# A three-block transformer kernel on one core: the experts' down products move into their own block's turn; in the second attention the rotary work goes ahead of the convolution's taps and sigmoid gates become tangents

## The chip, the cores and the metric

The kernel is one program on 1 core of a Trainium2 chip. The metric is the device time of one execution in microseconds (us), lower is better. The core has a matrix engine (TensorE, PE in the rows; PEld is its weight load), a vector engine (VectorE, DVE), an activation engine (ScalarE, ACT), GpSimd (POOL) and SyncE (SP), which here only issues transfers. They run side by side, each in its own written order, and wait for one another by semaphores.

## The reference, cut to what matters

Three transformer blocks stand one after the other on 512 tokens of width 1024. The change touches the mixture of experts of the first block and the attention with its convolution in the second.

```
# first block: mixture of experts
order = jnp.argsort(e_flat)                      # assignments sorted by expert, 32 experts, 2 per token
def run(args):
    xb, e = args
    gate, up = jnp.split(xb @ w_gate_up[e], 2, axis=-1)
    return (jax.nn.silu(gate) * up) @ w_down[e]
y = jax.ops.segment_sum(y_buf[dest] * w_s[:, None].astype(h.dtype), tok_s, num_segments=n_tok)

# second block: projections, attention over 8 heads in blocks of 128 queries, convolution of width 31
z = h @ w_in
c_q, c_kv, k_r, u_glu, gate_logits = jnp.split(z, IN_OFFSETS, axis=-1)
q = (rms_norm(c_q, q_norm) @ w_uq).reshape(B, S, N_HEADS, QK_NOPE_DIM + QK_ROPE_DIM)
q_rope = apply_rope(q[..., QK_NOPE_DIM:], cos[:, :, None, :], sin[:, :, None, :])
s = jnp.einsum('bhqd,bhkd->bhqk', qn_b, k_nope) + jnp.einsum('bhqd,bkd->bhqk', qr_b, k_rope)
p = jax.nn.softmax(s, axis=-1).astype(v.dtype)   # causal mask before it

a, b = jnp.split(u_glu, 2, axis=-1)
u = a * jax.nn.sigmoid(b)
u = lax.conv_general_dilated(u, conv_w, padding=[(CONV_WIDTH - 1, 0)], feature_group_count=CONV_CHANNELS) + conv_b
u = jax.nn.silu(layer_norm(u, conv_ln_g, conv_ln_b))
```

## The kernel before, in words

The kernel is one hand-ordered program for each engine. Every function such as `moe_pe` or `att2_dve` writes out one engine's part of a stage, and its order in the text is the order in which that engine works. A helper records operations for all of them, so the line in a row is often a helper's: L316 to L318 are the three products of a weight tile, L324 general products, L339 transposes, L294 and L302 the high and the low part of a weight tile.

**Weights in two parts.** A weight tile that must be multiplied exactly is split: ACT copies the rounded high part (`act_hi`, L294, tiles ws0h to ws2h), DVE subtracts it from the weight (`dve_lo`, L302, ws0l to ws2l), and PE multiplies high by high, high by low and low by high. `dve_lo` of a tile waits for its `act_hi`, and that waits until PE has finished the tile that held the same buffers.

**Experts.** The 32 experts are taken as 16 blocks of two (`NMAIN`), each expert on 64 rows. A turn of the loop is: gate and up products of block bb (L1535, 32 matmuls from `w` and the gathered tokens in `arena`), with 16 products back to the tokens (L324, `onehot`, `yo_hi`, `yo_lo`) of block bb - 2 between them; 8 transposes of the next block's tokens; silu on ACT (L1612), times up and the routing weight on DVE (L1637), 2 transposes of that on PE (L339 from `t`), a copy on ACT (L1616); then the 16 down products of block bb - 1 (L1535 from `w` and `t`). ACT and DVE split the outcome (L1606, L1628), and DVE adds what comes back to x (L1632). After the loop stand the 8 pairs of products back of block 14, the down products of block 15 and its 8 pairs back. Weights come on SP's queue, in the order gate-up, down, gate-up, down, 2 MB and 1 MB for an expert, into two rings of 5 buffers. A transfer into a ring's buffer waits until the products that last used it are done, and those behind it in the queue wait too.

**Second attention.** Its 32 units are 8 heads of 4 query blocks, i = 3, 2, 1, 0 (512, 384, 256, 128 keys). In step t of 35 PE makes the scores of unit t (L324), turns the probabilities of unit t - 2 (L2018) and multiplies those of unit t - 3 by the values; DVE has the reciprocal and a diagonal for unit t - 1 (L2066, L2069), the maximum for unit t (L2074), then `CONV2` taps of the convolution (L1864; the first tap of a channel group is L1861), then what the fills need, and at i = 0 the rotary part of the next head's query (`head2_dve`, L1981, L1982, L1984), for which the next head's first scores wait. The convolution has 8 groups of 31 taps, 248 in all.

**Fills.** The 16 tiles of u_glu are called fills. PE spreads the 24 matmuls of each over some three steps (L1935). Even fills are the gate's half, which ACT turns into the sigmoid (L1834). Odd fills are the other half, which DVE multiplies with it (L1846). Before an odd fill's product DVE catches up with taps until `31 * (m - 1)` are done. Fills 0 to 3 come ahead of the attention (`p2_pe`), fills 4 to 15 in steps 1, 4, 7, 10, 13, 16, 18, 21, 24, 27, 30 and 33. All those in the attention use one bank, so PE starts a fill only when its predecessor was taken. The taps left after the attention run between the first merge's tiles (`mixN_dve`, `ln_dve`: 20 after tile 0, 20 after tile 1, all the rest after tile 2).

## Time and profile before

| | |
|---|---|
| median of 3 runs | 2996.79 us (2995.47 to 3001.74) |
| profiled execution, its own time | 2995.61 us |
| its span | 2993.6 us |
| mean granted clock of TensorE | 0.943 |
| TensorE busy | 89% of the span |
| VectorE busy | 52% |
| ScalarE busy | 34% |
| expert loop, first gate product to last product back | 630.60 to 926.2 us |
| second attention, first scores to last | 1048.12 to about 1310 us |

A row of the trace gives start and duration in us, engine, line, operation, output and inputs with their shapes, how many instructions are merged in it, and in brackets how long the engine had been idle and what ended that.

### The profile page before, as it was taken

The numbers are of one execution on the slowest core, as the hardware profiler recorded it, in microseconds if no ns is written. First come the engines' busy times: TensorE is split into PE (matmuls) and PEld (weight loads), VectorE is DVE, ScalarE is ACT, GpSimd is POOL, SyncE is SP. The second block draws the span as 40 slices with busy tenths as digits, with TensorE's granted clock in tenths as the row PEclk, the third lists the DMA queues.
The fourth block names the chain that finished last, engine by engine and source line by source line (L and its number), as shares of the span: only waits on it lengthen the run. The fifth ranks groups of instructions, "written<-read, shape, count | busy, mean of one in ns | idle before, by whom it ended". The sixth has DMA issues, their size and how long they took to land.

```text
span 2993.6 us, 29418 instructions
## 1 busy us (share of the span) xinstructions
PE 2677.3 (89%) x11760; PEld 1923.5 (64%) x11760; DVE 1565.7 (52%) x2840; ACT 1010.6 (34%) x1723; POOL 15.8 (1%) x20
## 2 busy tenths in 40 slices
PE   6989998979994989978994999949989999999997
PEld 2566777633432645556873888837768878778786
DVE  5226764457557466778536444475553323343534
ACT  1024454321113322332433333324663334442232
POOL 0000000000000000000000000000000000000000
PEclk9988999989997988989997999979999999999999
DMA  6111002198982200021320232121213143122220
GB/s 176 42 43 31 29 15 85 57 372 358 371 358 84 88 22 15 15 85 56 113 105 35 85 113 85 57 71 61 68 57 113 57 112 86 69 85 85 85 83 31
DMA packets 178749, 295.99 MB, mean 99 GB/s; under 512 B 26160, under 2 KB 120752, under 8 KB 170416
## 3 DMA queue, kind: packets, MB, share of 16 engines
q1 hardware_dynamic: 175088, 282.52, 27.0%
q0 software_dynamic: 2304, 8.39, 0.7%
q10 hardware_dynamic: 1216, 3.15, 0.3%
q8 instruction: 95, 1.56, 0.2%
q14 instruction: 46, 0.38, 0.0%
HBM read 288.79 MB, written 4.19 MB: 98 GB/s over the span
## 4 chain that ended last, share of the span: by engine, by line
PE 54%; DVE 10%; ACT 3%; issue 1%; DVEq 0%; ACTq 0%
PE ps L316 15%; PE ps L318 15%; PE ps L317 15%; PE ps L324 7%; DVE arena L1864 3%; PE ps L1935 2%; DVE t L369 1%; DVE t L353 1%; PE ps L339 1%; DVE t L2186 0%; PE ps L2018 0%; DVE arena L2168 0%; PE ps L1957 0%; ACT L2595 0%; DVE ws0l L302 0%
## 5 line engine op out<-in xcount | busy, mean ns | idle before, releaser
L302 DVE TENSOR_TENSOR ws0l<-w,ws0h 128x1024 fp32r<-128x1024 f32 (+2 forms) x125 | 135.4, 1083 | 128.8 <-ACT ws0h L294 128.5
L302 DVE TENSOR_TENSOR ws1l<-w,ws1h 128x1024 fp32r<-128x1024 f32 (+1 forms) x124 | 137.7, 1110 | 119.1 <-ACT ws1h L294 119.1
L1864 DVE SCALAR_TENSOR_TENSOR arena<-arena 128x512 f32<-128x512 f32 x240 | 180.3, 751 | 7.4
L324 PE MATMUL ps<-arena 128*128 128x512 f32 (+11 forms) x440 | 145.4, 511 | 27.4 <-DVE arena L1984 23.0
L294 ACT ACTIVATE ws0h<-w 128x1024 fp32r<-128x1024 f32 (+2 forms) x125 | 117.8, 943 | 127.8 <-PE ps L318 124.0
L294 ACT ACTIVATE ws1h<-w 128x1024 fp32r<-128x1024 f32 (+1 forms) x124 | 119.4, 963 | 111.4 <-PE ps L318 104.3
L302 DVE TENSOR_TENSOR ws2l<-w,ws2h 128x1024 fp32r<-128x1024 f32 (+1 forms) x94 | 102.1, 1086 | 89.3 <-ACT ws2h L294 89.3
L1535 PE MATMUL ps<-w,arena 128*64 128x512 f32 x512 | 129.5, 643 | 20.4 <-issue 19.0
L324 PE MATMUL ps<-t,con 128*128 128x512 f32 (+1 forms) x68 | 46.1, 773 | 107.3 <-DVE t L353 86.7
L316 PE MATMUL ps<-hpc_hi,ws0h 128*128 128x512 f32 x320 | 128.1, 400 | 6.1 <-DVE ws0l L302 4.0
L316 PE MATMUL ps<-hpc_hi,ws1h 128*128 128x512 f32 x328 | 130.9, 399 | 1.5 <-issue 1.5
L318 PE MATMUL ps<-hpc_hi,ws1l 128*128 128x512 f32 x328 | 128.9, 393 | 0.0
L317 PE MATMUL ps<-hpc_lo,ws1h 128*128 128x512 f32 x328 | 128.7, 392 | 0.0
L316 PE MATMUL ps<-hpc_hi,ws2h 128*128 128x512 f32 x312 | 123.5, 396 | 3.3 <-ACT hpc_hi L1102 2.3
L317 PE MATMUL ps<-hpc_lo,ws0h 128*128 128x512 f32 x320 | 125.2, 391 | 0.0
L318 PE MATMUL ps<-hpc_hi,ws0l 128*128 128x512 f32 x320 | 125.2, 391 | 0.0
L339 PE MATMUL ps<-con,t 128*128 128x128 f32 (+1 forms) x556 | 102.4, 282 | 23.5 <-DVE t L982 7.3
L318 PE MATMUL ps<-hpc_hi,ws2l 128*128 128x512 f32 x312 | 121.6, 390 | 0.0
L317 PE MATMUL ps<-hpc_lo,ws2h 128*128 128x512 f32 x312 | 121.4, 389 | 0.0
L294 ACT ACTIVATE ws2h<-w 128x1024 fp32r<-128x1024 f32 (+1 forms) x94 | 88.7, 944 | 86.3 <-PE ps L318 86.3
L1632 DVE TENSOR_TENSOR x<-x,ps 128x512 f32<-128x512 f32 x128 | 80.4, 681 | 64.8 <-PE ps L324 64.7
L339 PEld LDWEIGHTS ps<-con,t 128*128 128x128 f32 (+1 forms) x556 | 70.7, 142 | 59.6 <-issue 10.7
(533 smaller groups left out, 6142.2 us busy)
## 6 DMA issues: line engine op xcount, KB each, us to landing
w<-in_w_gate_up SPq DMA_DIRECT2D x32, 2048.0 KB, 12.1
w<-in_w_in SPq DMA_DIRECT2D x37, 1024.0 KB, 5.6
w<-in_w_down SPq DMA_DIRECT2D x32, 1024.0 KB, 11.4
w<-in_w_ff SPq DMA_DIRECT2D x16, 2048.0 KB, 8.1
w<-in_w_in SPq DMA_DIRECT2D x13, 2048.0 KB, 7.8
w<-in_w_in SPq DMA_DIRECT2D x48, 512.0 KB, 5.2
w<-in_w_branch SPq DMA_DIRECT2D x6, 2048.0 KB, 7.7
w<-in_w_out SPq DMA_DIRECT2D x4, 2048.0 KB, 7.8
```

The lines of the kernel that those rows point to most:

```text
L294: A_(e).activation(pair_of(t)[0], tiles[t][1], ACT.Copy).then_inc(*e.inc(hi, ("hi", t)))
L302: e.go.tensor_tensor(p[1], tiles[t][1], p[0].bitcast(F32), ALU.subtract).then_inc(*e.inc(lo, ("lo", t)))
L316: e.go.matmul(bank, p[0][:, k, :], high, start=k == 0, stop=False)
L317: e.go.matmul(bank, p[0][:, k, :], low, start=False, stop=False)
L318: i = e.go.matmul(bank, p[1][:, k, :], high, start=False, stop=k == K - 1)
L324: i = e.go.matmul(bank, lt, rt, start=j == 0, stop=j == n - 1)
L339: i = e.go.transpose(dst, src, ident[0:k, 0:k])
L353: e.go.tensor_tensor(N.acc[:], N.acc[:], N.square(k)[:], ALU.add).then_inc(*e.inc(dv, (N.tag, "add", k)))
L1535: i = e.go.matmul(bank[h_, :], rows[:, h_], weights[r], start=start, stop=stop)
L1632: e.go.tensor_tensor(x[:, d, :], x[:, d, :], ps[3 + (8 * bb + d) % 3][:], ALU.add).then_inc(*e.inc(dv, ("xm", bb, d)))
L1864: i = e.go.scalar_tensor_tensor(out=cv[:, m, :], in0=ureg[:, m % 2, k:k + 512], scalar=cw[:, m, k:k + 1], in1=cv[:, m, :], op0=ALU.mult, o ...
L1935: i = e.go.matmul(ps[5][:], p[w_ // 2][:, k, :], hpN[w_ % 2][:, k, :], start=r == 0, stop=r == 23)
```

## The change

The experts' loop gets a different order on PE, ACT and DVE: the two gate transposes come ahead of the next tokens' eight, and the down products are those of the turn's own block. The products back are then those of block bb - 1, and the work after the loop shrinks to one block's. In the second attention the gate's sigmoid becomes a hyperbolic tangent of half the argument: sigmoid(b) = (tanh(b / 2) + 1) / 2, the 1 is added in the product on DVE, and the factor one half goes once into the convolution's weights. On DVE the low part of a weight tile two ahead is made before an odd fill's catch-up and product, the rotary part of the next head stands ahead of the taps, and a step has 6 taps for 5.

```diff
-                behind = {2: (0, 1, 2), 5: (3, 4, 5), 7: (6, 7)} if bb - 2 >= b0 else {}
+                behind = {2: (0, 1, 2), 5: (3, 4, 5), 7: (6, 7)} if bb > b0 else {}
                 for k in range(8):
...
                     for d in behind.get(k, ()):
-                        back(bb - 2, d)
+                        back(bb - 1, d)
+                e.wait_ge(*dv(("up", bb)))
+                turns(e, [(ps[2][:, P * k:P * k + P], tm[bb % 2][:, P * k:P * k + P]) for k in range(2)], ("g", bb))
                 if bb + 1 < b1:
                     turn_x(bb + 1)
-                e.wait_ge(*dv(("up", bb)))
-                turns(e, [(ps[2][:, P * k:P * k + P], tm[bb % 2][:, P * k:P * k + P]) for k in range(2)], ("g", bb))
-                if bb > b0:
-                    down(bb - 1)
-            for d in range(8):
-                back(b1 - 2, d)
-            down(b1 - 1)
+                down(bb)
             for d in range(8):
                 back(b1 - 1, d)
...
-                e.go.activation(sig_of(j)[:], fill_bank(j)[:], ACT.Sigmoid).then_inc(*e.inc(ev, ("fill", j)))
+                e.go.activation(sig_of(j)[:], fill_bank(j)[:], ACT.Tanh, scale=0.5).then_inc(*e.inc(ev, ("fill", j)))
...
             m = j // 2
+            dve_lo(e, fill_t[j] + 2)
             if j % 2:
                 while e.conv < 31 * (m - 1):
                     conv_dve(e, 1)
...
-                e.go.tensor_tensor(ureg[:, m % 2, 30:542], sig_of(j)[:], fill_bank(j)[:], ALU.mult).then_inc(*e.inc(dv, ("fill", j)))
+                e.go.scalar_tensor_tensor(out=ureg[:, m % 2, 30:542], in0=sig_of(j)[:], scalar=1.0, in1=fill_bank(j)[:], op0=ALU.add,
+                                          op1=ALU.mult).then_inc(*e.inc(dv, ("fill", j)))
                 e.inputs = m + 1
-            dve_lo(e, fill_t[j] + 2)
...
+                        e.go.tensor_scalar(cw, cw, 0.5, None, ALU.mult).then_inc(*e.inc(dv, "cw"))
...
-        CONV2 = 5
+        CONV2 = 6
...
+                if t < NU2 and units2[t][1] == 0 and units2[t][0] < 7:
+                    head2_dve(e, units2[t][0] + 1)
                 conv_dve(e, CONV2)
                 for j in fills_at(t):
                     fill_dve(e, j)
-                if t < NU2 and units2[t][1] == 0 and units2[t][0] < 7:
-                    head2_dve(e, units2[t][0] + 1)
```

ACT and DVE follow in the experts' loop: ACT copies the gates before the next tokens and takes the own block's outcome, and DVE makes the matrix back to the tokens (`to_tokens`, L1473, L1476) after its product with up.

On PE, the end of turn 1 of the experts' loop reads so before: the last gate product (weights in buffers `w_51` and `w_52`), the next tokens' transposes, the gates' transposes, then the down products of block 0 (`w_63`, `w_64`).

```order
L1535 MATMUL ps<-w_52,arena 64x512
L339 MATMUL ps<-con,arena 128x128 x8
L339 MATMUL ps<-con,t 128x128 x2
L1535 MATMUL ps<-w_63,t 64x512
L1535 MATMUL ps<-w_64,t 64x512
```

The same place now ends with a product back of block 0 (`onehot_90`), and the down products are those of block 1 (`w_65`, `w_66`).

```order
L324 MATMUL ps<-onehot_90,yo_lo 128x512
L339 MATMUL ps<-con,t 128x128 x2
L339 MATMUL ps<-con,arena 128x128 x8
L1535 MATMUL ps<-w_65,t 64x512
L1535 MATMUL ps<-w_66,t 64x512
```

The two sets of transposes have changed places, and each block's down products stand one turn earlier.

On DVE, steps 27 and 28 of the second attention read so before: the maximum of unit 27 (ISA, 128x128), the taps, the product of fill 13 (L1846), the low part for fill 15, the rotary part of head 7 (L1981 to L1984), the reciprocal and the diagonal, and the maximum of unit 28.

```order
L2074 ISA ps,m<-ps,con 128x128
L2074 ISA m 128x1
L1864 SCALAR_TENSOR_TENSOR arena<-arena 128x512 x6
L1846 TENSOR_TENSOR arena<-t,ps 128x512
L302 TENSOR_TENSOR ws1l<-w_59,ws1h 128x1024
L1981 TENSOR_TENSOR ps<-ps,tabs 64x512
L1982 TENSOR_TENSOR t<-t,tabs 64x512
L1984 TENSOR_TENSOR arena<-t,ps 64x512
L2066 RECIPROCAL m<-m 128x1
L2069 TENSOR_SCALAR tabs<-con,m 128x128
L2074 ISA ps,m<-ps,con 128x512
```

The same steps now (lines of the new file: L1973 to L1976 rotary, L1856 taps, L1834 the fill's product, L2066 the maximum):

```order
L2066 ISA ps,m<-ps,con 128x128
L2066 ISA m 128x1
L1973 TENSOR_TENSOR ps<-ps,tabs 64x512
L1974 TENSOR_TENSOR t<-t,tabs 64x512
L1976 TENSOR_TENSOR arena<-t,ps 64x512
L1856 SCALAR_TENSOR_TENSOR arena<-arena 128x512 x6
L302 TENSOR_TENSOR ws1l<-w_59,ws1h 128x1024
L1834 SCALAR_TENSOR_TENSOR arena<-t,ps 128x512
L2058 RECIPROCAL m<-m 128x1
L2061 TENSOR_SCALAR tabs<-con,m 128x128
L2066 ISA ps,m<-ps,con 128x512
```

The rotary part has moved ahead of the taps, and the fill's product behind the low part.

On ACT, a turn of the experts' loop reads so before: silu, the next block's tokens, the gates' copy, the high part of the down products, the next silu.

```order
L1612 ACTIVATE t<-ps 128x256
L1599 ACTIVATE arena<-ps 128x512 x2
L1616 ACTIVATE t<-ps 128x256
L1606 ACTIVATE yo_hi<-ps 128x512 x2
L1612 ACTIVATE t<-ps 128x256
```

And now, with L1608 for silu, L1610 for the copy, L1595 for the tokens and L1602 for the high part:

```order
L1608 ACTIVATE t<-ps 128x256
L1610 ACTIVATE t<-ps 128x256
L1595 ACTIVATE arena<-ps 128x512 x2
L1602 ACTIVATE yo_hi<-ps 128x512 x2
L1608 ACTIVATE t<-ps 128x256
```

The copy of the gates has moved ahead of the tokens' two copies. In the second block the program before has 7 loads of a table of functions ahead of L1834 and 7 ahead of the exponential (L2043); the new one has a single one, ahead of the first tangent.

## Rows read from the trace of the kernel before

**Rows 1.** Waits of PE, 640 to 930 us: total us, times, longest.

```profile
PE ps L1535 <- issue: 19.0, 9, 3.9
```

**Rows 2.** Timeline of PE in the experts' loop.

```profile
630.60 9.54 PE L1535 MATMUL ps<-w,arena 128*64 128x512 f32 x32 [0.78 <-ACT arena L1599]
...
642.28 7.09 PE L1535 MATMUL ps<-w,arena 128*64 128x512 f32 x32 [0.61 <-ACT t L1616]
...
854.71 3.65 PE L1535 MATMUL ps<-w,t 128*64 128x512 f32 x16
...
870.87 3.65 PE L1535 MATMUL ps<-w,t 128*64 128x512 f32 x16
877.43 4.49 PE L1535 MATMUL ps<-w,arena 128*64 128x512 f32 x12 [2.91 <-issue]
...
895.34 2.74 PE L1535 MATMUL ps<-w,arena 128*64 128x512 f32 x12
```

**Rows 3.** Timeline of all engines at the end of the experts' loop.

```profile
907.41 0.38 ACT L1616 ACTIVATE t<-ps 128x256 f32<-128x256 f32 x1 [1.11 <-PE ps L339]
...
917.36 3.65 PE L1535 MATMUL ps<-w,t 128*64 128x512 f32 x16
...
925.79 0.39 PE L324 MATMUL ps<-onehot,yo_lo 128*128 128x512 f32 x1
```

**Rows 4.** Windows, experts' loop: us, PE, PEld, DVE, ACT, POOL busy, clock, DMA share, GB/s.

```profile
711.00:727.00 16.00, 13.19 (x58) 5.86 (x58) 15.31 (x31) 1.47 (x3) 0.94 (x1) 1.00 0.97 402
...
823.00:837.00 14.00, 14.00 (x66) 6.40 (x64) 10.04 (x22) 2.35 (x5) 0.94 (x1) 1.00 1.02 429
```

**Rows 5.** Transfers, 640 to 900 us.

```profile
DMA packets 9896, 94.21 MB, mean 362 GB/s; under 512 B 1103, under 2 KB 1103, under 8 KB 2767
```

**Rows 6.** Waits of PE, 1048 to 1310 us.

```profile
PE ps L324 <- DVE arena L1984: 23.0, 8, 5.2
PE ps L1935 <- DVE arena L1846: 6.8, 3, 5.6
```

**Rows 7.** Timeline of PE in the attention: first scores of heads 6 and 7.

```profile
1257.64 1.12 PE L324 MATMUL ps<-arena 128*128 128x512 f32 x2 [2.48 <-DVE arena L1984]
...
1291.16 2.07 PE L324 MATMUL ps<-arena 128*128 128x512 f32 x2 [5.22 <-DVE arena L1984]
```

**Rows 8.** The chain of waits, same places: start, us, what.

```profile
1259.81 1.14 PE ps L1935 x4
...
1262.99 1.48 PE ps L324 x4
...
1295.24 2.00 PE ps L1935 x4
```

**Rows 9.** Timeline of DVE in the attention, head 6 to the first merge.

```profile
1282.38 0.30 DVE L2074 CUSTOM_DVE_ANT_0 ps<-ps,con 128x128 f32<-128x128 f32 x1 [3.94 <-PE ps L324]
...
1282.60 4.68 DVE L1864 SCALAR_TENSOR_TENSOR arena<-arena 128x512 f32<-128x512 f32 x6
...
1287.99 1.22 DVE L302 TENSOR_TENSOR ws1l<-w,ws1h 128x1024 fp32r<-128x1024 f32 x1
1289.12 0.68 DVE L1981 TENSOR_TENSOR ps<-ps,tabs 64x512 f32<-64x512 f32 x1
...
1291.04 0.15 DVE L2066 RECIPROCAL m<-m 128x1 f32<-128x1 f32 x1
...
1327.70 1.22 DVE L302 TENSOR_TENSOR ws2l<-w,ws2h 128x1024 fp32r<-128x1024 f32 x1
```

**Rows 10.** Timeline of PE at the first merge and ahead of the attention.

```profile
1034.41 5.53 PE L324 MATMUL ps<-arena,w 128*128 128x512 f32 x12 [1.05 <-DVE arena L1846]
...
1329.07 0.76 PE L316 MATMUL ps<-hpb_hi,ws2h 128*128 128x512 f32 x1 [9.59 <-DVE ws2l L302]
```

**Rows 11.** Timeline of ACT in step 31: a table load for the sigmoid.

```profile
1307.47 0.59 ACT L2052 ACTIVATE arena<-ps 128x512 f32<-128x512 f32 x1
1308.08 1.28 ACT L1834 ACT_TABLE_LOAD   x1
```

More of the change, by code:

```diff
@@ L1612, in moe_act @@
                 e.go.activation(tm[bb % 2][:, 0:256], ps[2][:, 0:256], ACT.Silu).then_inc(*e.inc(ev, ("silu", bb)))
+                e.wait_ge(*tp(("g", bb)))
+                e.go.activation(tm[bb % 2][:, 256:512], ps[2][:, 0:256], ACT.Copy).then_inc(*e.inc(ev, ("g", bb)))
                 if bb + 1 < b1:
                     turned_x(bb + 1)
-                e.wait_ge(*tp(("g", bb)))
-                e.go.activation(tm[bb % 2][:, 256:512], ps[2][:, 0:256], ACT.Copy).then_inc(*e.inc(ev, ("g", bb)))
-                if bb > b0:
-                    high(bb - 1)
+                high(bb)
                 if bb == 6:
                     act_sines(e, "a2", 0)
-            high(b1 - 1)
         def moe_dve(e, b0, b1):
@@ L1644, in moe_dve @@
             for bb in range(b0, b1):
-                old = range(8) if bb - 2 >= b0 else ()
+                old = range(8) if bb > b0 else ()
                 for d in old[0:3]:
-                    add(bb - 2, d)
+                    add(bb - 1, d)
                 if bb + 2 < b1:
@@ L1651, in moe_dve @@
                 for d in old[3:6]:
-                    add(bb - 2, d)
-                if bb > b0:
-                    to_tokens(e, bb - 1)
+                    add(bb - 1, d)
                 up(bb)
                 for d in old[6:8]:
-                    add(bb - 2, d)
+                    add(bb - 1, d)
+                to_tokens(e, bb)
                 if bb + 1 < b1:
                     weights_of(e, bb + 1)
-                if bb > b0:
-                    low(bb - 1)
+                low(bb)
                 if bb == 4:
@@ L1666, in moe_dve @@
                     dve_angles(e, "a2", 0, tm[4][:], tm[4][:], tm[5][:])
-            for d in range(8):
-                add(b1 - 2, d)
-                if d == 2:
-                    to_tokens(e, b1 - 1)
-            low(b1 - 1)
             for d in range(8):
@@ L1859, in conv_dve @@
                     e.wait_ge(*dv(("fill", 2 * m + 1)))
-                    e.wait_ge(*in_cw("cw"))
+                    if m == 0:
+                        e.wait_ge(*in_cw("cw"))
+                        e.go.tensor_scalar(cw, cw, 0.5, None, ALU.mult).then_inc(*e.inc(dv, "cw"))
+                    e.wait_ge(*dv("cw"))
                     i = e.go.tensor_scalar(cv[:, m, :], ureg[:, m % 2, 0:512], cw[:, m, 0:1], vcol("conv_b_2", m), ALU.mult, ALU.add)
```

## The prediction

> **What bounds the kernel now.** I read the busy shares first: TensorE works 89% of the span, so time is made or lost where it stops. Then I read, for the two stages that the change touches, the waits of PE, and the timelines around the longest.
>
> In the experts' loop PE waits 9 times, 19.0 us in all, for something that the waits put down to "issue" [rows 1]. The name says little; the place says more. The waits stand ahead of the first gate product of a block, which waits for the weights to land (one is the 2.91 us) [rows 2]. The queue explains it. Down products of block bb - 1 end a turn, and until then their buffer holds up the down transfer and the three behind it: 6.3 MB start together, and the last is needed one turn later. A turn without such a wait is 870.87 - 854.71 = 16.2 us, down products to down products [rows 2]; 6.3 MB at 0.42 MB/us take 15 us, and a landing is not instant. So now transfer and turn run neck and neck, and the transfers stop between two lots: the mean over the loop is 362 GB/s [rows 5], while windows inside a lot have 402 and 429 [rows 4]. After a wait the products also run slower: 12 of them take 4.49 us behind the wait of 2.91, and 2.74 otherwise [rows 2].
>
> In the attention PE waits 23.0 us in 8 places for the rotary part of the next head's query and 6.8 us in 3 for the product of an odd fill [rows 6]. DVE is not full there. It has the taps ahead of what PE wants: 6 taps from 1282.60, product, low part, and only at 1289.12 the rotary part [rows 9], while PE stood from 1285.94 to 1291.16 [rows 7].
>
> **The experts' loop.** Nothing is added or removed, only moved. In turn 0 the gate products end at 640.1, and the next gate product, which waited for the gates' copy, began at 642.28 [rows 2]; now block 0's down products begin there, say 642.5, and take 3.5, so turn 1 begins at 646.0 (642.28 before).
>
> From then on a turn is 16.2 us plus what the new order exposes. The down products now want the copy that ACT makes after PE's two gate transposes. At the loop's end, where nothing follows those, the copy runs from 907.41 to 907.79 [rows 3], 0.5 us with its handing over; in other turns the next tokens' 8 transposes lie over it. The cost is between 0 and 0.5; as most is covered I take 0.2: 16.4 us a turn. One turn is longer for another reason: DVE makes the second block's angles, and in that window it is busy 15.3 of 16 us and PE idle 2.8 [rows 4]. I keep 2.4 for it. Turn 15 begins at 646.0 + 14 x 16.4 + 2.4 = 878.0, against 895.34 [rows 2].
>
> The tail: from that start to the copy's end are 907.8 - 895.3 = 12.5 us, from the last down products to the last product back 926.2 - 917.4 = 8.8 [rows 3]. The down products of block 14 and its 8 pairs back, which stood between, are gone. The loop ends at 899.3 instead of 926.2: **26.9 us less**.
>
> Does the queue keep up? A turn needs 6.29 MB of weights and 0.52 MB of gathered tokens. At 429 GB/s that is 15.9 us, at 402 it is 16.9 [rows 4]. Now two thirds of a turn's weights start with the own block's down products, and the last gate-up with the gate products' end, 22 us before it is needed and not 16; and at the start there is a lead: the last weights of turn 3 are issued at about 657, land by 663, and turn 3 begins at 679. At 16.9 us a turn 14 turns use up 7 of these 16. So I count no wait. The lower bound is the mean of 362 [rows 5] staying as it is: 18.8 us a turn, 34 us more over 14 turns less the lead of 16: a gain of 9. The upper bound is 0 exposed: 30.
>
> The Trainium skill, DMA: Bandwidth & Descriptors, in its opening table, puts HBM's share of one core at about 358 GB/s. By that a turn would be 19.0 us, an estimate, and the loop would gain some 5 us. The windows' 402 and 429 speak against it for a core that runs alone, as the page's own section on its measurements does.
>
> **Ahead of the attention.** At fill 3 the product now stands behind the low part of a tile, which waits for PE's end of fill 3, for ACT's high part (about as long as the low) and then takes 1.1 itself (1289.12 - 1287.99 [rows 9]). PE waits for the product there already, 1.05 us [rows 10]. So + 2.1 us.
>
> **The attention, until unit 27's maximum.** Two heads' first scores are at 1257.64 and 1291.16; less the wait of 5.22 that is 28.3 us of PE work for a head [rows 7]. From 1048.1 to unit 27 at 1282.4 [rows 9] are 6 x 28.3 + 24.6 = 194.4 us of such work, 24.6 being a head up to its last scores. The stretch lasts 234.3: 39.9 are lost. Some 16 are waits for the rotary part (23.0 less the last, 5.2, and the first, which end outside), 6.8 for products [rows 6]. Nearly all the rest is the clock: after some waits the scores take 2.07 us where they else take 1.12, twice, and 4 products of a fill 2.00 and not about 1.1 [rows 7, 8], some 3 us each time, about five times.
>
> With the change the rotary part starts behind the maximum and takes 1.9 [rows 9], and PE wants it 3.7 after unit 27's scores, by 1285.94: no wait. But DVE now has, from the maximum of a head's last unit (0.1 behind the scores): 0.35, rotary 1.9, 6 taps of 0.79 (4.7), reciprocal and diagonal 0.45. So the next maximum comes at 7.6, while its scores end at 5.9 (3.7 and 2 x 1.12 [rows 7]). Over a head DVE has 24 taps, 18.9, maxima and diagonals some 4.2, rotary 1.9, fills some 2: 27 of 28.3. It keeps up but is late in a head's first two steps, and there an odd fill's product is late too. Fill 5 (step 4): maximum at 7.6, seven taps, low part, product: done 15.5. PE wants it behind the next scores, which end 6.8 after the first's start (1264.47 - 1257.64 [rows 7, 8]): at 10.5, wait 5.0. Fill 9 (step 16) likewise with six taps: 4.3. Fill 11 (step 21): 0.7. Fill 7: none. That is 10.0 us, with two clock losses after the long ones, 6, and the one of the first head, 3: 19 lost where 39.9 were. **20.9 us less**; bounds: nothing late, 34 less, and each wait doubled with its clock, 8 less.
>
> **From unit 27 to the first merge** DVE sets the pace: 1282.4 to 1327.70, when the merge's low part starts [rows 9], for which PE waits 9.59 [rows 10]. It gets 8 x 6 = 48 taps for 8 x 5 and 2 of catch-up: 6 more, 4.7 us. It loses its wait for the scores that its own rotary part held up, from about 1291.5 until 2 x 2.07 after 1291.16 [rows 7], 3.7. With what its pauses leave: + 1.2.
>
> **The merge.** 37 taps are left, not 57: 20, 17, 0 after the first three tiles instead of 20, 20, 17. PE waits for the first two lots; the third lies beside its products. 3 x 0.79: 2.4 less.
>
> **Tables.** 13 loads of 1.28 us go from ACT [rows 11]. PE's waits in the attention are DVE's, 29.8 us [rows 6]; the loads lie beside other work, and I count nothing for them. The Trainium skill, ScalarE: Activation LUTs, section "What ACT_TABLE_LOAD costs", adds a drain of 1.38 us to each. Here the copy before a load ends at 1308.06 and the load begins at 1308.08 [rows 11]: no such gap. With the drain 13 x 2.66 us would leave ACT, and the sum would still be the same. The tangent's product in place of the plain one, and one scaling of 248 columns, are under 0.5 us beside a DVE wait.
>
> **The sum.** - 26.9 + 2.1 - 20.9 + 1.2 - 2.4 = - 46.9. The profiled execution took 2995.6 us, 1.2 under the median of the runs: 2995.6 - 46.9 = 2948.7, and on the median's scale **2950**.
>
> **The rivals.**
> 1. The stream binds the experts' loop (for it: the windows reach 402 only with pauses around; against: the lead). Gain there 9, not 27: 2968. Chance 0.12.
> 2. DVE binds the attention: it has 27 of 28.3 us a head, so small delays may add up, fills of every step be late, and the clock fall more often. The attention gives 2, not 21: 2969. Chance 0.16. With rival 1: 2987, 0.03.
> 3. PE waits for no fill, as ACT and DVE find slack that I don't see: the attention gives 34: 2937. Chance 0.08.
> 4. Slower than before: each turn of the experts now has a short wait for the copy, and if the clock fell after each, at 3 us of slower products and 1 of wait, 14 turns would be 56 us longer, in all 3006. It decides from 3.4 us a turn. Rows of short waits speak against it: behind the 0.61 of 642.28, 32 gate products took 7.09 us, the full clock's time [rows 2]. Chance 0.02.
>
> My forecast, all near its terms, has 0.57: 2938 to 2962 by its bounds. The range 2936 to 2974 takes in rivals 1, 2 and 3 and leaves their sum and rival 4 out. A measurement of this kernel tells 0.2%, 6 us, from no change. All cases but rival 4 are faster by more; I leave 0.02 for cases between.
>
> **What would show it.** In the new profile: experts' turns of 16.4 us, no wait named issue at L1535, a granted clock of 1.0, the loop's end near 899; no wait of PE for L1976, but waits of 4 to 5 us for L1834 in steps 5 and 17; the wait at the first merge some 10 us; one table load in the attention. Wrong it would be if turns of 18 us stayed, or DVE were without any pause from the first head on.

## The result and the profile after

| | before | changed |
|---|---|---|
| median of the runs | 2996.13 us (4 runs, 2994.26 to 3001.74) | 2943.65 us (4 runs, 2940.32 to 2948.74) |
| profiled execution, its span | 2995.61, 2993.6 us | 2946.20, 2944.2 us |
| mean granted clock | 0.943 | 0.946 |

The ratio is 0.9824, with a 95% interval from 0.9805 to 0.9843: the median is 52.5 us lower, and 6 us below the forecast's 2950. By stretches of the two profiled executions (us; "maximum" is DVE's for unit 27, "low part" DVE's ws2l at the first and at the third tile of the merge):

| stretch | before | changed | difference | forecast |
|---|---|---|---|---|
| start to first gate product | 630.6 | 628.1 | -2.5 | 0 |
| experts' loop | 295.6 | 270.2 | -25.4 | -26.9 |
| to the first scores | 121.9 | 125.4 | +3.5 | +2.1 |
| to unit 27's maximum | 234.3 | 209.9 | -24.4 | -20.9 |
| to the first low part | 45.3 | 45.0 | -0.4 | +1.2 |
| to the third low part | 48.3 | 47.6 | -0.7 | -2.4 |
| rest | 1617.6 | 1618.2 | +0.5 | 0 |

The lines below are those of the new file: L1608 silu, L1610 the gates' copy, L1626 the sum into x, L1821 the tangent, L1834 the fill's product, L1853 and L1856 taps, L1927 fills on PE, L1973 to L1976 rotary, L2066 the maximum.

The waits of PE from 640 to 900 us, which answer to [rows 1] (what it waited for, total us, times, longest):

```profile
PE ps L324 <- DVE x L1626: 4.1, 2, 3.7
PE ps L1535 <- ACT t L1610: 0.6, 1, 0.6
```

The wait named issue is gone. The long one that is left, 3.72 us, comes from DVE, in the turn in which it makes the angles. The timeline of PE shows it, and a plain turn for comparison; the last row is the last block's down products, ahead of which the gates' copy lies bare:

```profile
705.56 3.65 PE L1535 MATMUL ps<-w,t 128*64 128x512 f32 x16
...
719.82 0.79 PE L324 MATMUL ps<-onehot,yo_hi 128*128 128x512 f32 x1 [3.72 <-DVE x L1626]
...
726.95 3.65 PE L1535 MATMUL ps<-w,t 128*64 128x512 f32 x16
...
743.24 3.65 PE L1535 MATMUL ps<-w,t 128*64 128x512 f32 x16
...
889.45 3.65 PE L1535 MATMUL ps<-w,t 128*64 128x512 f32 x16 [0.56 <-ACT t L1610]
```

From down products to down products are 16.3 us (743.24 - 726.95), in the turn of the angles 21.4. The transfers from 640 to 860 us, answering to [rows 5], no longer pause between two lots; over the same 220 us the kernel before had a mean of 364 GB/s:

```profile
DMA packets 9578, 90.77 MB, mean 413 GB/s; under 512 B 1063, under 2 KB 1063, under 8 KB 2726
```

One slice of 5.5 us still has 182 GB/s, in the turn of the angles, and all others have 381 or more.

Ahead of the attention, at the norm behind the loop, PE waits less for a sum of DVE than before. The first row is the kernel before from 926 to 1048 us, the second the changed one from 898 to 1023:

```profile
PE ps L324 <- DVE t L353: 25.5, 2, 14.8
PE ps L324 <- DVE t L353: 23.2, 2, 14.8
```

The waits of PE from 1000 to 1300 us, answering to [rows 6]:

```profile
PE ps L316 <- DVE ws2l L302: 13.7, 1, 13.7
PE ps L1927 <- DVE arena L1834: 12.1, 3, 5.0
PE ps L324 <- DVE arena L1834: 3.3, 1, 3.3
PE ps L324 <- DVE arena L1976: 2.1, 1, 2.1
PE ps L1927 <- ACT t L1821: 0.6, 1, 0.6
```

Of the 23.0 us for the rotary part 2.1 are left, those ahead of the very first scores. The timeline of PE has the places of the others; the first row answers to [rows 10], the second to fourth are the products of fills 5, 9 and 13 (the last of these behind unit 27), and the last row is the wait at the first merge:

```profile
1007.12 8.40 PE L324 MATMUL ps<-arena,w 128*128 128x512 f32 x12 [3.26 <-DVE arena L1834]
...
1064.91 0.76 PE L1927 MATMUL ps<-hpb_hi,ws0h 128*128 128x512 f32 x1 [5.02 <-DVE arena L1834]
...
1155.78 0.47 PE L1927 MATMUL ps<-hpb_hi,ws0h 128*128 128x512 f32 x1 [3.82 <-DVE arena L1834]
...
1242.24 0.77 PE L1927 MATMUL ps<-hpb_hi,ws0h 128*128 128x512 f32 x1 [3.21 <-DVE arena L1834]
...
1279.86 0.77 PE L316 MATMUL ps<-hpb_hi,ws2h 128*128 128x512 f32 x1 [13.65 <-DVE ws2l L302]
```

DVE at the head's change (its timeline, answering to [rows 9]) takes the rotary part right behind the maximum, and has no pause up to the next maximum (the reciprocal and the diagonal stand in the last gap):

```profile
1205.20 0.30 DVE L2066 CUSTOM_DVE_ANT_0 ps<-ps,con 128x128 f32<-128x128 f32 x1 [3.08 <-PE ps L324]
...
1206.75 0.68 DVE L1976 TENSOR_TENSOR arena<-t,ps 64x512 f32<-64x512 f32 x1
1207.36 4.68 DVE L1856 SCALAR_TENSOR_TENSOR arena<-arena 128x512 f32<-128x512 f32 x6
...
1212.35 0.69 DVE L2066 CUSTOM_DVE_ANT_0 ps<-ps,con 128x512 f32<-128x512 f32 x1
```

### The profile page after: what moved, and what is told of

The parts are those of the page before. It is cut to its first block, busy times and chain, and to the rows that moved or that the text cites. A ratio compares the mean times of both kernels' runs of the same rounds, so it can differ in the third digit from the quotient of the medians.

```text
span 2944.2 us, 29406 instructions
## 1 busy us (share of the span) xinstructions
PE 2663.1 (90%) x11760; PEld 1919.8 (65%) x11760; DVE 1565.4 (53%) x2841; ACT 993.5 (34%) x1710; POOL 15.3 (1%) x20
## 4 chain that ended last, share of the span: by engine, by line
PE 56%; DVE 9%; ACT 3%; issue 1%; DVEq 0%; ACTq 0%
PE ps L316 15%; PE ps L318 15%; PE ps L317 15%; PE ps L324 7%; DVE arena L1856 2%; PE ps L1927 2%; DVE t L369 1%; DVE t L353 1%; PE ps L339 1%; PE ps L1949 0%; DVE t L2179 0%; PE ps L2010 0%; ACT L2588 0%; DVE arena L2161 0%; DVE ws0l L302 0%
## 5 line engine op out<-in xcount | busy, mean ns | idle before, releaser
L1856 DVE SCALAR_TENSOR_TENSOR arena<-arena 128x512 f32<-128x512 f32 x240 | 180.2, 751 | 7.3
L324 PE MATMUL ps<-t,con 128*128 128x512 f32 (+1 forms) x68 | 45.7, 767 | 102.6 <-DVE t L353 84.2
L317 PE MATMUL ps<-hpc_lo,ws0h 128*128 128x512 f32 x320 | 125.4, 392 | 0.0
L318 PE MATMUL ps<-hpc_hi,ws0l 128*128 128x512 f32 x320 | 125.4, 392 | 0.0
L1535 PE MATMUL ps<-w,arena 128*64 128x512 f32 x512 | 122.3, 611 | 0.8 <-ACT arena L1595 0.8
L316 PE MATMUL ps<-hpb_hi,ws0h 128*128 128x512 f32 x168 | 70.9, 422 | 40.0 <-DVE ws0l L302 27.8
```

The source lines that it names most:

```text
L316: e.go.matmul(bank, p[0][:, k, :], high, start=k == 0, stop=False)
L317: e.go.matmul(bank, p[0][:, k, :], low, start=False, stop=False)
L318: i = e.go.matmul(bank, p[1][:, k, :], high, start=False, stop=k == K - 1)
L324: i = e.go.matmul(bank, lt, rt, start=j == 0, stop=j == n - 1)
L1535: i = e.go.matmul(bank[h_, :], rows[:, h_], weights[r], start=start, stop=stop)
L1856: i = e.go.scalar_tensor_tensor(out=cv[:, m, :], in0=ureg[:, m % 2, k:k + 512], scalar=cw[:, m, k:k + 1], in1=cv[:, m, :], op0=ALU.mult, o ...
```

## The experiments

Twelve kernels ran, in three groups of four, each group on one chip beside the kernel before. Medians, ratios to the kernel before in the same group, and the stretches of each one's profile in the order of the table above (us):

| run | median | ratio, 95% interval | start | loop | to scores | to unit 27 | to merge | merge |
|---|---|---|---|---|---|---|---|---|
| experts only | 2972.3 | 0.9919 (0.9897 to 0.9940) | 636.9 | 271.3 | 119.1 | 240.3 | 45.7 | 48.5 |
| second block only | 2968.8 | 0.9914 (0.9882 to 0.9947) | 625.1 | 294.6 | 127.1 | 212.4 | 45.3 | 46.1 |
| queue order | 2986.0 | 0.9970 (0.9948 to 0.9991) | 639.3 | 269.1 | 122.6 | 240.5 | 45.9 | 48.6 |
| angles in two | 2941.8 | 0.9817 (0.9784 to 0.9849) | 635.8 | 264.8 | 125.4 | 209.9 | 46.6 | 46.7 |
| low part behind | 2939.9 | 0.9801 (0.9753 to 0.9850) | 637.1 | 271.0 | 119.1 | 207.2 | 44.7 | 46.2 |
| rotary behind | 2981.0 | 0.9949 (0.9922 to 0.9975) | 641.8 | 269.0 | 121.3 | 241.6 | 49.1 | 46.0 |
| five taps | 2942.1 | 0.9821 (0.9776 to 0.9865) | 625.0 | 270.9 | 121.3 | 213.6 | 41.7 | 49.0 |
| gates behind | 2961.0 | 0.9882 (0.9835 to 0.9930) | 630.7 | 282.9 | 125.4 | 210.0 | 46.5 | 46.7 |
| changed, again | 2941.6 | 0.9838 (0.9802 to 0.9873) | 631.4 | 270.5 | 121.3 | 208.6 | 46.5 | 46.7 |
| sigmoid | 2939.8 | 0.9825 (0.9801 to 0.9849) | 625.3 | 271.3 | 121.2 | 209.8 | 46.0 | 46.4 |
| early products | 2921.9 | 0.9772 (0.9748 to 0.9796) | 625.4 | 271.1 | 119.1 | 197.6 | 45.1 | 44.8 |
| early products, angles in two | 2919.4 | 0.9753 (0.9728 to 0.9778) | 624.1 | 264.9 | 118.8 | 200.6 | 45.1 | 44.5 |

The column "start" is code that no kernel changes, and it varies by 18 us. Totals are therefore read with their intervals, and the stretches say where an edit acts.

**The parts of the change.** First, the experts' functions of the changed kernel in the kernel before (the hunks of the diff in `moe_pe`, `moe_act`, `moe_dve`), then everything but them:

```diff
 # experts only: before, with
-                        back(bb - 2, d)
+                        back(bb - 1, d)
...
+                down(bb)
```

> The kernel before with the experts' part of the change alone. My theory, from the two traces (the loop lasts 295.6 us before and 270.2 after, of 25.4 between them nothing comes from elsewhere): 25 us less than the kernel before, 2971, and a loop with turns of 16.3 us. Rival: part of what the loop gains is lost again behind it, as transfers for the second block then come closer together; then 20 us less or fewer.

```diff
 # second block only: before, with
-        CONV2 = 5
+        CONV2 = 6
...
+                    head2_dve(e, units2[t][0] + 1)
                 conv_dve(e, CONV2)
```

> The changed kernel with the experts' functions of the kernel before, so the second block's part alone. The stages' differences add up to 3.5 more ahead of the attention, 24.4 less until unit 27's maximum, 1.1 less to the end of the merge: 22 less than before, 2974. If the two parts help one another (the experts' part lets the second block's weights come sooner), this and the run with the experts' part alone give together clearly less than the 52.5 us of the whole change.

The medians are 22.1 and 25.6 below the kernel before's 2994.39. Together 47.7, where the whole change has 52.5 and, in its second run, 51.5 (2993.11 - 2941.6): the two parts add up, within what the intervals allow, and neither needs the other. The loop alone has 24.3 us less, the attention alone 21.8. The first run's interval, 18 to 31 us less, cannot tell the 25 of the theory from the 20 of its rival.

The attention's gain depends on which execution it is read against. Its old code took 234.3 us in the kernel before, but 240.3 with the new experts' loop and 240.5 in the next run; for the same 825 matmuls PE was busy 210.7, 215.4 and 218.5 us, at a clock of 0.92, 0.90 and 0.89. Against those two the changed kernel's 209.9 is some 30 us less and not 24. One profile of each does not tell whether the shorter loop has a part in that.

**What the loop waited for.** The theory was that the waits named issue come from the order in SP's queue, not from the order on PE. This run leaves PE, ACT and DVE as they were and issues the gate-up weights of a block ahead of the down weights of the one before it:

```diff
         for h_ in range(2 * NB):
-            expert_w = []
-            for w_, ring_, n in ((wgu, GU_SLOT, 4096), (wdn, DN_SLOT, 2048)):
...
+            for b_ in range(b0_, b1_ + 1):
+                order_ += [(0, 2 * b_ + r) for r in range(2) if b_ < b1_]
+                order_ += [(1, 2 * b_ - 2 + r) for r in range(2) if b_ > b0_]
+        for kind, h_ in order_:
...
```

> The kernel before with nothing moved on PE, ACT or DVE: only SP's queue issues the experts' slabs in another order, gate-up of block b, then down of block b - 1. So no gate-up transfer stands behind a down transfer whose buffer is late. My theory, that the block in the queue makes the waits of 19.0 us ahead of the gate products: the 9 waits and the slow clock behind them go, turns of 16.2 to 16.5 us, 13 to 20 us less than before, 2977 to 2983; the rest up to 25 is the shorter tail. Rival, that the stream itself cannot keep up, or that a down buffer's release sets the pace in any order: the waits stay, 0 to 3 us less.

All 9 waits are gone. The waits of PE from 640 to 908 us:

```profile
PE ps L324 <- DVE x L1637: 5.8, 4, 3.7
PE ps L1540 <- ACT arena L1604: 0.8, 1, 0.8
PE ps L1540 <- ACT t L1621: 0.6, 1, 0.6
```

Turns are 16.1 us, as its down products show:

```profile
809.54 3.65 PE L1540 MATMUL ps<-w,t 128*64 128x512 f32 x16
...
825.67 3.65 PE L1540 MATMUL ps<-w,t 128*64 128x512 f32 x16
```

The loop takes 269.1 us, 26.5 less than before and no more than in the changed kernel. So the queue's order alone is enough for the loop's whole gain, and PE's new order is one way among others to get it. How the queue stood still is seen in the timeline of SP in the kernel before: four transfers (the first and the last are shown) are issued in one breath when the down products that began at 854.71 [rows 2] end, then none for 15 us:

```profile
858.43 0.33 SPq L3014 DMA_DIRECT2D w<-in_w_down  x1
...
859.75 0.72 SPq L3014 DMA_DIRECT2D w<-in_w_gate_up  x1
874.59 0.33 SPq L3014 DMA_DIRECT2D w<-in_w_down  x1
```

In the changed kernel the last gate-up transfer comes apart from the others, in the middle of the turn:

```profile
844.61 0.33 SPq L3007 DMA_DIRECT2D w<-in_w_down  x1
...
854.96 0.33 SPq L3007 DMA_DIRECT2D w<-in_w_gate_up  x1
860.88 0.33 SPq L3007 DMA_DIRECT2D w<-in_w_down  x1
```

The Trainium skill, DMA: Bandwidth & Descriptors, section "Anatomy of one DMA — SWDGE (gpsimd) path", says in a note, on any DMA, that a wait on a semaphore is taken on the issuing sequencer before it dispatches, and the DMA engines only work off what is in their queues. The rows of SP agree: while SP waits for a down buffer, gate-up transfers whose buffers are free are not issued.

The total moved less than the loop: 8.4 us, between 3 and 16 by its interval, where 13 to 20 were expected. As the interval ends at 16 and the loop has 26.5, at least some 10 us were lost elsewhere. In its profile the start is 8.7 longer and the attention 6.3 (240.5 against 234.3), both in unchanged code, at lower clocks. Part of this can't be the edit: the run with the experts only, whose start and attention are those of the kernel before too, has 6.3 and 6.0 more there. But the run with the experts only kept 22.1 of its loop's 24.3 us in its median, and this one 8.4 of 26.5. Whether the transfers' new order itself costs something outside the loop stays open.

**The angles.** Their two halves in turns 4 and 5:

```diff
+        def dve_angles(e, tag, w, pos, ang, kk, parts=(0, 1)):
...
-                    dve_angles(e, "a2", 0, tm[4][:], tm[4][:], tm[5][:])
+                    dve_angles(e, "a2", 0, tm[4][:], tm[4][:], tm[5][:], (0,))
+                if bb == 5:
+                    dve_angles(e, "a2", 0, tm[4][:], tm[4][:], tm[5][:], (1,))
```

> The changed kernel with the second block's angles on DVE made in two halves, one in turn 4 of the experts and one in turn 5. In the changed kernel turn 5 lasts 21.4 us where the others have 16.27, and PE waits there 3.7 us for a sum of DVE. My theory, that all 5.1 come from this work standing in one place: half of it fits into what DVE has free in a turn, 3 to 5 us less than the changed kernel. Rival, that DVE has no 2 us free in a turn: the same loss in two pieces, 0 to 1 less.

The long turn is 17.1 us and not 21.4 (in the changed kernel's second profile 22.7), the one behind it 16.3, from down products to down products:

```profile
712.23 3.65 PE L1538 MATMUL ps<-w,t 128*64 128x512 f32 x16
...
729.34 3.65 PE L1538 MATMUL ps<-w,t 128*64 128x512 f32 x16
```

The windows from the first of the two turns' gate products on (us; PE, PEld, DVE, ACT, POOL busy; clock; DMA share; GB/s) have DVE busy 14.9 of 16.2 and 14.5 of 16.3 us, PE busy nearly throughout, and the clock full:

```profile
715.70:731.90 16.20, 15.81 (x72) 6.51 (x70) 14.91 (x30) 3.01 (x6) 0.94 (x1) 1.00 1.00 415
731.90:748.20 16.30, 16.30 (x76) 7.03 (x74) 14.54 (x31) 3.09 (x7) 0.94 (x1) 1.00 0.99 402
```

The loop takes 264.8 us, 5.4 less: the theory held. It is too small for the totals alone (2941.8, and 2941.6 to 2943.7 for the changed kernel).

**The low part's place.**

```diff
-            dve_lo(e, fill_t[j] + 2)
             if j % 2:
...
                 e.inputs = m + 1
+            dve_lo(e, fill_t[j] + 2)
```

> The changed kernel with one step undone: the low part of the weight tile two ahead stands again behind an odd fill's product. The changed kernel waits 12.1 us in 3 places for products of fills 5, 9 and 13 and 3.3 us for that of fill 3. My theory, that the low part (1.2 us and its own wait for ACT's high part) stands in front of each product: each wait is 1.1 to 1.3 us shorter, 4 to 5 us in all, and 1 to 3 more if the slow clock ahead of the first scores goes too; 4 to 8 less than the changed kernel, some 2938. Rival, that PE needs the low part as much as the product: no gain, the wait moves to the weights.

The waits of PE from 1000 to 1279 us have 3.3 us less for fills 5, 9 and 13, and 2.2 less for fill 3:

```profile
PE ps L1927 <- DVE arena L1833: 8.8, 3, 4.0
...
PE ps L324 <- DVE arena L1833: 1.1, 1, 1.1
```

From the loop's end to unit 27 it takes 326.3 us, 3.7 less than the changed kernel in its second profile (121.3 + 208.6) and 9.0 less than in its first. So in the stretches this step of the change costs some 4 us, and the attention's gain comes from its other steps. The medians (2939.9, against 2943.7 and 2941.6) agree but are too close to show it; 4 to 8 us were expected.

**The rotary part's place.**

```diff
-                if t < NU2 and units2[t][1] == 0 and units2[t][0] < 7:
-                    head2_dve(e, units2[t][0] + 1)
                 conv_dve(e, CONV2)
...
+                if t < NU2 and units2[t][1] == 0 and units2[t][0] < 7:
+                    head2_dve(e, units2[t][0] + 1)
```

> The changed kernel with the rotary part of the next head again behind the taps and the fill's product. My theory, that its place alone brings the attention's gain: PE waits again 18 to 23 us for it, more than in the kernel before by 0.8 a head for the sixth tap, and the attention until unit 27's maximum takes 234 to 242 us against 209.9: 22 to 30 more than the changed kernel, 2966 to 2974. Rival, that the tangent, without table loads on ACT, brings a part of the gain: then 10 to 18 more.

The attention takes 241.6 us: all of its gain is gone (234.3 in the kernel before, 240.3 with the experts only). The waits of PE from 1030 to 1300 us:

```profile
PE ps L324 <- DVE arena L1976: 28.0, 8, 5.0
PE ps L1927 <- DVE arena L1834: 4.2, 2, 2.5
```

The waits for products shrink from 12.1 to 4.2, since PE is late itself. With the tangents in place no gain is left, so none of it came from them. The total is 37 to 39 above the changed kernel's two medians, beyond the 22 to 30 expected: in the profile 32 more in the attention and 4 up to the merge, and the unchanged start is 14 longer (641.8), of which the stretches ahead of the attention give back 5.

**Five taps for six.**

```diff
-        CONV2 = 6
+        CONV2 = 5
```

> The changed kernel with 5 taps a step as before, for 6. By my steps: waits for fills 5, 9 and 13 shorter by 0.8 to 1.6 each (3), from unit 27 to the first merge 6 taps less, 4.7 us, the merge 2.4 longer (57 taps left for 37): 3 to 6 less than the changed kernel, 2938 to 2941. Rival, that the catch-up ahead of products takes back what the steps save, and the merge pays for every tap: 0 to 6 more.

Both theories were half right, and the sum is nothing (2942.1 against 2941.6 and 2943.7). The stretch to the merge is 3.2 us shorter than in the changed kernel's first profile and 4.8 than in its second, the merge 1.5 or 2.3 longer; 4.7 and 2.4 were expected. But the attention is 3.8 or 5.0 longer, where I had expected 3 less: the wait for fill 5 grew from 5.02 us, and there is one for fill 11, which six taps had not. PE's timeline:

```profile
1059.39 0.77 PE L1927 MATMUL ps<-hpb_hi,ws0h 128*128 128x512 f32 x1 [7.39 <-DVE arena L1834]
...
1192.34 0.47 PE L1927 MATMUL ps<-hpb_hi,ws0h 128*128 128x512 f32 x1 [2.78 <-DVE arena L1834]
```

DVE's timeline has the reason for the first. Fill 5's product wants 31 taps done in any case. With five a step, 25 are, and the other six are made behind the low part, right ahead of the product:

```profile
1048.81 3.90 DVE L1856 SCALAR_TENSOR_TENSOR arena<-arena 128x512 f32<-128x512 f32 x5
1052.62 1.22 DVE L302 TENSOR_TENSOR ws1l<-w,ws1h 128x1024 fp32r<-128x1024 f32 x1
1053.76 4.68 DVE L1856 SCALAR_TENSOR_TENSOR arena<-arena 128x512 f32<-128x512 f32 x6
1058.55 0.69 DVE L1834 SCALAR_TENSOR_TENSOR arena<-t,ps 128x512 f32<-128x512 f32 x1
```

**The gates' copy laid bare.** It tests rival 4, by making the short wait of each turn longer. This is PE's part; ACT's copies are put back likewise:

```diff
+                if bb + 1 < b1:
+                    turn_x(bb + 1)
                 e.wait_ge(*dv(("up", bb)))
                 turns(e, [(ps[2][:, P * k:P * k + P], tm[bb % 2][:, P * k:P * k + P]) for k in range(2)], ("g", bb))
-                if bb + 1 < b1:
-                    turn_x(bb + 1)
                 down(bb)
```

> The changed kernel with the next tokens' transposes again ahead of the gates', on PE and ACT, the down products still in their own block's turn. So PE has nothing to do between the gates' transposes and the down products, which wait for ACT's copy. It tests my rival 4. Theory: each turn has a wait of 0.5 to 0.8 us and the clock stays at its full level, turns of 16.8 to 17.1 us, 8 to 12 more than the changed kernel, 2952 to 2956. Rival 4: the clock falls behind each such wait, turns of 18 to 20 us, 30 to 55 more.

PE now waits 16 times for the copy, as its waits from 640 to 914 us show:

```profile
PE ps L1535 <- ACT t L1612: 13.6, 16, 0.9
```

Turns are 17.1 us for 16.3, and the granted clock stays full through them. The window from 760 to 780 us, with a whole turn in it (us; PE, PEld, DVE, ACT, POOL busy; clock; DMA share; GB/s):

```profile
760.00:780.00 20.00, 19.11 (x89) 8.59 (x86) 13.43 (x29) 2.95 (x6) 0.94 (x1) 1.00 0.99 404
```

Rival 4 is refuted for waits of this length. The loop is 12.7 us longer, 0.85 a turn, a little over the upper end of the theory. The total is 5 us over the expected 2952 to 2956; in the profile the turn of the angles, 23.8 us for 21.4, and the unchanged start, 2.6 longer, have as much.

**The changed kernel again, and the sigmoid.**

> The changed kernel once more, on the chip of this group, to compare the next three with. By the earlier runs: 2938 to 2946. Its stretches in this second profile show which of the differences are the program's and which are the clock's: the experts' loop should be the same within 1 us, the 12 products ahead of the attention either 8.4 us (as in the changed kernel's profile) or 5.5 (as with 5 taps).

The loop is the same within 0.3 us. The 12 products ahead of the attention take 5.5 us here, behind the same wait:

```profile
1009.50 5.53 PE L324 MATMUL ps<-arena,w 128*128 128x512 f32 x12 [3.27 <-DVE arena L1834]
```

So 2.9 of the first profile's 125.4 us in this stretch are the clock. Of the eight profiles with this wait of 3.3 us four have 8.2 to 8.4 us for these products and four 5.5; all six with a wait of 1.05 have 5.5. That speaks for the longer wait as the reason, in some executions and not in others; eight against six profiles do not prove it. Where the clock does not fall, the step's own difference is plain: 121.3 us here, and 119.1 in the run with the experts only, whose code ahead of the attention is that of the kernel before.

The next run has the sigmoid and the plain product again, and scales the convolution's weights by 1:

```diff
-                e.go.activation(sig_of(j)[:], fill_bank(j)[:], ACT.Tanh, scale=0.5).then_inc(*e.inc(ev, ("fill", j)))
+                e.go.activation(sig_of(j)[:], fill_bank(j)[:], ACT.Sigmoid).then_inc(*e.inc(ev, ("fill", j)))
...
-                e.go.scalar_tensor_tensor(out=ureg[:, m % 2, 30:542], in0=sig_of(j)[:], scalar=1.0, in1=fill_bank(j)[:], op0=ALU.add,
-                                          op1=ALU.mult).then_inc(*e.inc(dv, ("fill", j)))
+                e.go.tensor_tensor(ureg[:, m % 2, 30:542], sig_of(j)[:], fill_bank(j)[:], ALU.mult).then_inc(*e.inc(dv, ("fill", j)))
...
-                        e.go.tensor_scalar(cw, cw, 0.5, None, ALU.mult).then_inc(*e.inc(dv, "cw"))
+                        e.go.tensor_scalar(cw, cw, 1.0, None, ALU.mult).then_inc(*e.inc(dv, "cw"))
```

> The changed kernel with the sigmoid on ACT and the plain product on DVE as before (the convolution's weights scaled by 1). It brings back 7 loads of a table ahead of the sigmoid and 7 ahead of the exponential. My theory, that they lie beside other work: 0 to 3 us more than the changed kernel. Rival, that with the rotary part out of the way ACT is now next: an even fill's sigmoid comes 1.3 us or more later, the fill behind it waits, the clock falls: 8 to 20 more.

The medians are 2939.8 and 2941.6 (whose six runs lie between 2934 and 2965), no difference that can be told, though the loads are back (groups of ACT by line, 1000 to 1300 us):

```profile
L2034 ACT ACT_TABLE_LOAD x7 | 9.0, 1283 | 0.1
L1821 ACT ACT_TABLE_LOAD x6 | 7.7, 1283 | 0.1
```

PE waits 2.9 us in 2 places for the sigmoid, and 0.6 in one for the tangent. Only 0.9 of the 2.9 lies ahead of unit 27, and the attention takes 209.8, with the tangent 209.9 and 208.6.

**The products early.** Step 4's product wants 31 taps, so taps go where DVE waited for scores, 1.22 us ahead of the maximum of unit 2 and 2.85 ahead of that of unit 3; and the products go ahead of taps that nothing waits for. The low part stands behind the product again:

```diff
-            dve_lo(e, fill_t[j] + 2)
...
+            dve_lo(e, fill_t[j] + 2)
...
-                conv_dve(e, CONV2)
+                n = CONV2 + {1: 1, 2: 3}.get(t, 0)
+                first = {4: 3, 16: 1, 21: 3, 27: 2}.get(t, n)
+                conv_dve(e, first)
                 for j in fills_at(t):
                     fill_dve(e, j)
+                conv_dve(e, n - first)
```

> The changed kernel with the low part behind the product, one tap more in step 1 and three more in step 2 (where DVE waits 1.22 and 2.85 us for scores), and in steps 4, 16, 21 and 27 the fill's product ahead of most of the step's taps. Theory: the waits of 12.1 us in 3 places fall to 0 to 3 us and two falls of the clock with them, 3.3 ahead of the attention becomes 1.1; 10 to 16 less than the changed kernel, 2927 to 2934. Rival, that DVE's load sets the pace: the waits come back at the next maxima or at the first merge, 0 to 5 less.

It is 19.7 us below the changed kernel of the same group, 2921.9 against 2941.6, more than expected: the attention takes 197.6 us against 208.6, the stretch ahead of it 2.3 less, each part of the merge 1.4 to 1.9 less, and the unchanged start 6.0, which is chance, so the part above the expected 16 is not shown to be the edit's. From its first scores to unit 27 PE waits once:

```profile
1015.54 1.53 PE L324 MATMUL ps<-arena 128*128 128x512 f32 x2 [2.09 <-DVE arena L1976]
1052.82 0.47 PE L1927 MATMUL ps<-hpb_hi,ws0h 128*128 128x512 f32 x1 [0.86 <-DVE arena L1833]
```

The rival was right in one thing: behind unit 27 a wait comes up for an even fill's tangent. ACT has it behind a unit's exponential, that waits for DVE's maximum, and DVE had no pause before it.

```profile
1236.26 0.77 PE L1927 MATMUL ps<-hpb_hi,ws1h 128*128 128x512 f32 x1 [4.57 <-ACT t L1821]
```

**Both.** The same, with the angles in two:

```diff
+                if bb == 5:
+                    dve_angles(e, "a2", 0, tm[4][:], tm[4][:], tm[5][:], (1,))
...
+                first = {4: 3, 16: 1, 21: 3, 27: 2}.get(t, n)
```

> The kernel with the fills' products early, and the angles over two of the experts' turns. If the two gains are of different stages they add up: 4.3 to 5.4 us (turn 5 from 21.4 to 17.1, as the run with the angles alone showed) below the run with the early products alone, 2922 to 2930.

2919.4 us, 2.5 below the run before it, which the totals alone do not tell from nothing, and short of the expected 4.3 to 5.4. The loop has its gain, 6.2 us, and the attention took 2.9 more in this profile, with the same waits in it. It is the best of the kernels, 73.7 us below the kernel before of its group.

## Why the prediction was right

One more row of the kernel before, its turn of the angles, bears on the third point:

```profile
712.01 2.80 PE L1535 MATMUL ps<-w,arena 128*64 128x512 f32 x12 [2.38 <-issue]
```

- **The bound of the experts' loop.** Right, and now shown: the queue, not the stream, held up the weights. My reading of [rows 2] named it, and the queue's order alone removes the waits. Rival 1 (0.12) is refuted: the transfers keep 413 GB/s over 13 turns. But the stream has little to spare: the queue order's window from 720 to 860 us has 425 GB/s with a DMA share of 1.01, by which the 6.81 MB of a turn take 16.0 us, an estimate, and no turn in the middle of a loop here is shorter than 16.1. (The gain of some 5 us that I named for turns of 19.0 us is 6.5 by the sum that gives rival 1 its 9.)
- **A turn of 16.4 us.** Measured 16.27. The queue order's turns, in which no copy lies bare, are 16.15, so the new order exposes 0.12 where I took 0.2.
- **The angles, 2.4 us.** Mis-sized: 5.1 to 6.4. I had read PE's idle time of 2.8 us from a turn at whose start PE stood 2.38 us for its weights (the row above), in which DVE could catch up. There its longest wait for DVE was 1.12 us. Without the wait for weights it is 3.72, and the products back behind it take 0.63 us each and not 0.40. With turn 1 beginning 15.9 after the start and not 15.4, and the shorter turns, that makes -25.4 for my -26.9.
- **Ahead of the attention, +2.1.** The step is right: the wait went from 1.05 to 3.26, and 121.3 against 119.1 us are 2.2. Two things were in no term. The clock falls behind the longer wait in half of the profiles, 2.9 us, and behind the short one in none. And with the new loop the norm behind it starts sooner: ACT's first squares begin 1.6 us after the last product back and not 3.9, and PE's wait is 23.2 and not 25.5 us, in all eleven profiles with the new loop against all three with the old one. These 2.3 us are a gain of the experts' part that I did not foresee; why DVE lets ACT go sooner, no run shows.
- **The attention, -20.9.** Mechanism right, size 3.5 short. Waits of 5.02 and 3.82 were forecast as 5.0 and 4.3, none at fill 7 was right, the 0.7 at fill 11 did not come. The stretch is 209.9 where 194.4 is work: 15.5 are lost for my 19, of which 8.8 are waits (10.0) and 6.6 the clock and the rest, for which I had put 9. The 3.5 hold against the one profile of 234.3; where the old code took 240, the gain is some 30 us, still inside my bounds of 8 and 34. Rival 2 (DVE the bound) and rival 3 (no waits) did not come about. Rival 3's condition was then made by hand: with the products early the stretch loses 3.2.
- **The wait for fill 13, 3.2 us,** in step 28, was in no term. It lies behind unit 27, where DVE sets the pace anyway.
- **To the first merge +1.2, the merge -2.4.** Measured -0.4 and -0.7, in the second profile +1.2 and -1.6. The wait at the merge is 13.65 and not 10: DVE's work there is as long as I had it, but PE comes to it earlier, 32.7 us behind unit 27's maximum and not 37.1.
- **Tables: nothing.** Right, by the sigmoid's run.
- **The 6 us more than forecast** are only in part the program's. The two profiled executions differ by 49.4 us, 2.5 more than the forecast's 46.9: the attention has 3.5 and the unchanged start 2.5 more, and the other stretches give back 3.5. The remaining 3 us are that the changed kernel's profiled execution is 2.5 us above its median, the kernel before's 0.5 below.
- **Luck** has a small part. The loop gained 1.5 us less than forecast, and the unforeseen 2.3 behind it made up for that; and how near the attention's 20.9 come depends on the execution that it is read against.

## What to carry to other kernels

When a wait is put down to nothing in particular and stands ahead of a weight's first use, look at the issuing queue: which transfer's buffer is released last, and what stands behind it. Reordering the queue adds nothing on the engines, and here it gave the same loop as moving the products, though the total followed by only 8.4 of the loop's 26.5 us, so read the total too. On an engine that is nearly full, the order is the lever: put first what another engine waits for (here the rotary part was worth 32 us of the attention's time, the products another 11), then fill its pauses with the work that nobody waits for; a tap moved into a pause also pays for the catch-up that stands ahead of a later product.

## What was unexpected of the hardware

The granted clock is not the same from one execution to the next in code that nothing touched. In the window from 200 to 240 us it was 0.74 in the changed kernel (same columns as above):

```profile
200.00:240.00 40.00, 32.48 (x149) 23.06 (x148) 25.90 (x82) 20.70 (x61) 0.00 (x0) 0.74 0.09 27
```

In the run with the queue's order it was 0.54 in the same window:

```profile
200.00:240.00 40.00, 32.48 (x111) 22.00 (x112) 19.49 (x57) 18.03 (x48) 0.00 (x0) 0.54 0.09 27
```

PE is busy for the same 32.48 us in both, with 149 matmuls in the one and 111 in the other. The first gate product began anywhere from 624 to 642 us in 14 profiles. And the ten runs of the queue order's kernel lie in steps: four from 2976.5 to 2977.7 us at a mean clock of 0.943, five from 2986.0 to 2988.4 at 0.938 to 0.940, one at 2999.6 at 0.935. A gain of under 10 us has to be read from its stretch.
